# Squares of x in PSUM, the next layer's first slab on a buffer of its own, and a DRAM copy cut into eight, in a two-layer decoder kernel

## The reference

```python
def rms_norm(x, g):
    return x * rsqrt(mean(x * x, axis=-1) + EPS) * g

for layer in range(2):
    h = rms_norm(x, attn_norm[layer])
    x = x + (dsa_mixer(h, ...) if layer == 0 else swa_mixer(h, ..., sinks, ..., rel_bias))
    h = rms_norm(x, ffn_norm[layer])
    g, u = split(h @ w_gate_up[layer], 2)
    x = x + (silu(g) * u) @ w_down[layer]
out = rms_norm(x, final_norm)
```

## Time and profile before

| | us |
|---|---|
| median of 3 runs | 1193.57 (1193.28 to 1193.68) |
| profiled execution | 1198.54 |
| its span | 1196.7 |
| TensorE busy | 1166.6 (97%) |
| GpSimd busy | 613.7 (51%) |
| VectorE busy | 564.2 (47%) |
| ScalarE busy | 458.7 (38%) |

### The profile page before, as it was taken

How to read it: one execution, slowest core, us unless ns; L and a number is a source line. 1 busy time by engine, 2 the same in 40 slices (tenths; PEclk the granted TensorE clock), 3 DMA queues, 4 the chain that set the end, 5 groups by cost and what they waited for, 6 DMA issues and landing times.

```text
span 1196.7 us, 16183 instructions
## 1 busy us (share of the span) xinstructions
PE 1166.6 (97%) x5666; PEld 968.0 (81%) x5666; DVE 564.2 (47%) x931; ACT 458.7 (38%) x854; POOL 613.7 (51%) x359
## 2 busy tenths in 40 slices
PE   7999999999999999999999999999999999999997
PEld 5767889988788888888888778887888888888887
DVE  5389867644644344432222376737543444331111
ACT  5343257763423322323222376734333223322332
POOL 4435747864445444543444578824554445444441
PEclk9999999999999999999999999999999999999999
DMA  7531401118332333223332442313323332323331
GB/s 211 172 134 57 137 27 45 53 40 173 105 95 80 105 105 95 80 83 97 95 94 87 106 114 56 80 35 107 98 79 105 105 96 79 94 72 97 96 96 71
DMA packets 181571, 112.46 MB, mean 94 GB/s; under 512 B 7340, under 2 KB 175591, under 8 KB 181528
## 3 DMA queue, kind: packets, MB, share of 16 engines
q1 hardware_dynamic: 180800, 110.68, 33.2%
q10 hardware_dynamic: 728, 1.22, 0.3%
HBM read 109.72 MB, written 8.45 MB: 99 GB/s over the span
## 4 chain that ended last, share of the span: by engine, by line
PE 84%; DVE 5%; issue 2%; DMA 2%; ACT 2%; POOL 1%; ACTq 0%; SPq 0%; DVEq 0%
PE ps L576 26%; PE ps L578 26%; PE ps L577 26%; DMA raw<-in_ffn_w_gate_up 2%; PE ps L585 2%; DVE ss L1482 1%; PE ps L791 1%; DVE work L1578 1%; ACT w_hi L1090 1%; PE ps L967 1%; PE ps L770 1%; POOL w_lo L467 1%; DVE work L1562 1%; DMA raw<-in_b_w_in 1%; PE ps L970 0%
## 5 line engine op out<-in xcount | busy, mean ns | idle before, releaser
L467 POOL TENSOR_TENSOR w_lo<-raw,w_hi 128x1024 fp32r<-128x1024 f32 (+1 forms) x200 | 462.8, 2336 | 500.2 <-ACT w_hi L1090 491.7
L576 PE MATMUL ps<-xs_hi,w_hi 128*128 128x512 f32 (+3 forms) x1024 | 400.4, 391 | 8.0 <-DVE x L1678 2.9
L578 PE MATMUL ps<-xs_hi,w_lo 128*128 128x512 f32 (+3 forms) x1024 | 395.9, 387 | 0.0
L577 PE MATMUL ps<-xs_lo,w_hi 128*128 128x512 f32 (+3 forms) x1024 | 395.8, 387 | 0.0
L1090 ACT CAST w_hi<-raw 128x1024 fp32r<-128x1024 f32 (+1 forms) x196 | 178.9, 961 | 437.0 <-PE ps L578 415.6
L576 PEld LDWEIGHTS ps<-xs_hi,w_hi 128*128 128x128 f32 x1024 | 193.2, 189 | 53.6 <-issue 3.4
L577 PEld LDWEIGHTS ps<-xs_lo,w_hi 128*128 128x128 f32 x1024 | 193.3, 189 | 39.1 <-issue 1.1
L578 PEld LDWEIGHTS ps<-xs_hi,w_lo 128*128 128x128 f32 x1024 | 193.2, 189 | 39.0
L576 PE MATMUL ps<-act_hi,w_hi 128*128 128x512 f32 (+1 forms) x374 | 143.0, 382 | 0.0
L578 PE MATMUL ps<-act_hi,w_lo 128*128 128x512 f32 (+1 forms) x374 | 141.7, 379 | 0.0
L577 PE MATMUL ps<-act_lo,w_hi 128*128 128x512 f32 (+1 forms) x374 | 140.4, 375 | 0.0
(11 more groups left out here) (189 smaller groups left out, 1363.1 us busy)
## 6 DMA issues: line engine op xcount, KB each, us to landing
raw<-in_ffn_w_gate_up SPq DMA_DIRECT2D x88, 512.0 KB, 4.9
raw<-in_ffn_w_down SPq DMA_DIRECT2D x32, 384.0 KB, 3.6
raw<-in_a_w_in SPq DMA_DIRECT2D x20, 512.0 KB, 5.0
raw<-in_ffn_w_down SPq DMA_DIRECT2D x32, 320.0 KB, 4.0
raw<-in_b_w_in SPq DMA_DIRECT2D x10, 512.0 KB, 5.2
bias_toep<-bias_row SPq DMA_DIRECT2D x4, 1024.0 KB
toep<-bias_toep SPq DMA_DIRECT2D x16, 256.0 KB, 2.7
raw<-in_a_w_out SPq DMA_DIRECT2D x8, 512.0 KB, 4.1
```

Of the source, the lines that this page charges most:

```text
L467: nc.gpsimd.tensor_tensor(pieces(w_lo, n)[half], pieces(raw, n)[half], pieces(w_hi, n)[half].bitcast(F32), ALU.subtract)\
L576: nc.tensor.matmul(dst, wh, xh, start=start, stop=False, **kw)
L577: nc.tensor.matmul(dst, wh, xl, start=False, stop=False, **kw)
L578: return nc.tensor.matmul(dst, wl, xh, start=False, stop=stop, **kw)
```

## The change

- `new_x` writes the square of a tile to a PSUM bank (`NORM_SQ`, two banks for each norm) and adds from there. The very last half tiles still use `sq_mem`.
- Slab S_BK is loaded into a buffer of its own, `raw_next`, behind the tenth down slab of layer 0, and counted on a semaphore of its own. It lies over `gate`, `up` and `glu`, so its load waits for the last `act_lo`. Slab 55 takes its former slot, and waits for the split of slab 51; waits on `raw_full` of odd slabs behind S_BK count one slab less.
- The copy of the second bias table is cut into eight DMAs of two heads each (256 rows of 1 KB), one behind each of the down slabs 3 to 10 of layer 0. To that end the loop over the first five of eight output tiles (`AHEAD`) is written out on SyncE, in both layers.
- The sinks are loaded behind the first two slabs of queries.

```diff
+AHEAD = 5
+NORM_SQ = {1: (4, 5), 2: (2, 3), 3: (5, 7), 4: (2, 3)}
...
+        raw_next = sb("raw_next", [P, SLOT], F32, next_m)
...
+            if buf is raw and n == S_BK:
+                return [raw_next[:, 0:CUT_WIDE[0]], raw_next[:, CUT_WIDE[0]:CUT_WIDE[1]]]
...
             def slab(n, it, src):
                 for dst, s in src(n % 2):
-                    if n >= 2:
+                    if n == S_BK + 2:
+                        sp.wait_ge(lo_done, 2 * (S_BK - 1))
+                    elif n >= 2:
                         sp.wait_ge(lo_done, 2 * (n - 1) + 4 * it)
...
+            def row_copy(h):
+                sp.wait_ge(neg_done, 4 * H)
+                skew_b = bass.AP(tensor=bias_row.tensor, offset=h * GLEN + ROW_A + P - 1,
+                                 ap=[[GLEN, 2], [-1, P], [1, 2 * P]])
+                sp.dma_start(bias_toep[h:h + 2, :, 0:2 * P], skew_b).then_inc(toep_out, 16)
...
-                with sp.Fori(0, DM) as m:
+                for m in range(AHEAD):
+                    for c in range(2):
+                        slab(s_d + c, m, down(w_down[layer], c, m))
+                        if layer == 0 and m >= 1:
+                            row_copy(2 * (2 * (m - 1) + c))
+                if layer == 0:
+                    v = raw_next[:, :].rearrange("p (k n) -> p k n", k=DM)
+                    g = b_w_in[0].rearrange("(k p) n -> p k n", p=P)
+                    sp.wait_ge(al_done, FT)
+                    for i in range(2):
+                        sp.dma_start(v[:, 4 * i:4 * i + 4, :], g[:, 4 * i:4 * i + 4, H * DH:H * DH + 256])\
+                            .then_inc(raw_ahead, 16)
+                with sp.Fori(AHEAD, DM) as m:
                     for c in range(2):
                         slab(s_d + c, m, down(w_down[layer], c, m))
...
-            sp.wait_ge(neg_done, 4 * H)
-            skew_b = bass.AP(tensor=bias_row.tensor, offset=ROW_A + P - 1, ap=[[GLEN, H], [-1, P], [1, 2 * P]])
-            sp.dma_start(bias_toep[:, :, 0:2 * P], skew_b).then_inc(toep_out, 16)
             feed_forward(0, S_F0, S_D0)
-            slab(S_BK, 0, wide(b_w_in[0], H * DH))
-            sp.wait_ge(unit_done, U_BK)
-            sp.dma_start(sink[:, :], b_sinks[0:1, :].broadcast_to([P, H])).then_inc(sink_in, 16)
             for n in range(S_BQ, S_BO):
                 c0 = (n - S_BQ) * 2 * DH
                 slab(n, 0, two_halves(b_w_in[0], c0, c0 + H // 2 * DH))
+                if n == S_BQ + 1:
+                    sp.wait_ge(unit_done, U_BK)
+                    sp.dma_start(sink[:, :], b_sinks[0:1, :].broadcast_to([P, H])).then_inc(sink_in, 16)
...
-            sp.wait_ge(toep_out, 80)
+            sp.wait_ge(toep_out, 64 + 8 * 16)
...
-                    act.wait_ge(raw_full[n % 2], 32 * (n // 2 + 1) + 32 * it)
+                    if n == S_BK:
+                        act.wait_ge(raw_ahead, 32)
+                    else:
+                        act.wait_ge(raw_full[n % 2], 32 * (n // 2 + 1 - (n > S_BK and n % 2)) + 32 * it)
...
-                nc.scalar.activation(sq[:, par, :], x[:, m, :], ACT.Square).then_inc(sq_done, 1)
+                nc.scalar.activation(ps[:, NORM_SQ[e][par], :], x[:, m, :], ACT.Square).then_inc(sq_done, 1)
...
-                nc.vector.tensor_tensor(ss[:, :], ss[:, :], sq[:, par, :], ALU.add).then_inc(ss_done, 1)
+                nc.vector.tensor_tensor(ss[:, :], ss[:, :], ps[:, NORM_SQ[e][par], :], ALU.add).then_inc(ss_done, 1)
```

More of the change, by code:

```diff
@@ L213, in trunk @@
         act_lo = sb("act_lo", [P, FT, T], F32R, fm)
+        next_m = ExitStack()
+        raw_next = sb("raw_next", [P, SLOT], F32, next_m)
+        next_m.close()
         gate = sb("gate", [P, T], F32, fm)
@@ L230, in trunk @@
         raw_full = [sem("raw_full0"), sem("raw_full1")]
+        raw_ahead = sem("raw_ahead")
         hi_done, lo_done = sem("hi_done"), sem("lo_done")
```

## The result

The changed kernel takes 1185.41 us (median of 5, 1184.47 to 1187.31) against 1193.56 before on the same chip: a ratio of 0.9937, with a 95% interval from 0.9915 to 0.9959. That is 8.15 us less; forecast were 8.2 and 1185.3. The profiled executions lie 11.5 us apart (spans 1196.7 and 1185.2).

A forecast was written before the change was run, and what follows sets the result against it. TensorE, busy for 97% of the span, bounds the kernel, with losses at the seams between stages. Gains of 4.76 + 3.08 + 0.4 = 8.2 us off the median 1193.57 gave 1185.3 us, range 1183.6 to 1189.5.

The forecast's parts named there:

- Seam 1: Attention A to feed-forward 0: TensorE waits for x of tile 5 behind the bias copy; moving the copy gains 4.76 us.
- seam 2: Feed-forward 0 to attention B: the sinks hold up slab 54; loading them behind slabs 54 and 55 gains 3.08 us.
- seam 3: Attention B to feed-forward 1: wait of 0.5 us on the last x's low part; adding squares from PSUM gains 0.4 us.
- slow add: VectorE's add of squares beside a GpSimd split, 2.88 us; Seam 1 and seam 2 were to close even with it.
- quick add: VectorE's same add of squares, taken from PSUM: 0.69 us.
- sits there long before: Before attention B: slab 53 is in raw_next long before slab 54 lands at 661.4; no gain of its own was given.
- (c): Rival: squares gain nothing in PSUM, the add stays at 2.88 us; only 0.4 us lost, 1185.7 us; no chance given.
- The cover in the down part: Feed-forward 0's down slabs can come 10.3 us late without stalling TensorE; the copy pieces' cost taken as nothing, barely.
- backlog: Two DMA engines: piece plus down slab 7.9 to 8.4 us against 7.55; 3 to 7 us behind after eight.
- rival (f): More gain: in the stage behind seam 2 one return from the lower clock falls away, 1.7 us; 1183.6 us; 4%.

## Why the prediction was right, point by point

**The sum.** Seam 1 4.76, seam 2 3.08, seam 3 0.4: measured 4.77, 3.08 and 0.42 in the profiled executions. The total time came out 0.1 us from the forecast, which is luck: the runs scatter by more, and the kernel before had medians of 1193.79 to 1195.25 in the later comparisons.

**Where seam 1's credit belongs.** The chain that I read (copy, slab 15, cast, slow add, x of tile 5) was right link by link, and so was the claim that moving the copy closes it. The step that failed was to see only one cure: I had put the add's 2.2 us beside it ("even with the slow add"), but not asked what the quick add does while the slab stays late. The runs show that moving the copy removes the pause but for 0.26 us, and that the quick add does so too or leaves up to 0.6 us, which is all that the copy's place is then worth.

**Seam 2.** Right: the sinks alone. What I wrote of raw_next ("sits there long before") is true and worth nothing.

**The squares.** As (c) said, they matter little once the DMAs are moved: 0.26 + 0.4 us. I had seam 1's part at nothing, because I asked only whether the last add ends before the sum and left out the last low part, which is due 6 steps earlier. VectorE's timeline of before had it:

```profile
312.33 0.75 DVE L1473 SCALAR_TENSOR_TENSOR xs_lo<-x,params,xs_hi  x1 [1.18 <-ACT xs_hi L1105]
```

It ends 9.4 us after the cast at 303.71, so at 308.7 by the prediction's times, and TensorE needs it at 299.28 + 42 x 0.2275 = 308.8. That is no margin to speak of, and it came 0.26 us late.

**The cover in the down part.** The mechanism and the number of engines were right; the term for the backlog was mis-sized. During a piece the queue shows (571 to 573.5: packets, MB, share of 16 engines):

```profile
q1 hardware_dynamic: 118, 0.12, 13.6%
```

118 packets in 2.5 us on two engines: one each 42.4 ns per engine, while their busy time is 46 ns. Packets overlap by 4 ns, and I had added up busy times: 5.9 and 2.5 us instead of 5.4 and 2.1. So a cycle is 7.5 us against a period of 7.55, and no backlog grows. The tightest slab, the one behind raw_next, was asked for at 595.6 and 596.2; landings of its halves and its cast:

```profile
DMA to landing us min/median/max: 4.5/5.8/7.1
```
```profile
606.23 1.46 ACT L1119 CAST w_hi<-raw 128x768 fp32r<-128x768 f32 x2 [4.98 <-PE ps L604]
```

It was in place at 603.3, 3.1 us later than usual instead of 6 to 10, and 2.9 before its cast. With 42.5 ns in place of 46, the doubled pieces came out right too. The cut itself was not needed, as the copy left whole showed.

**Two engines, always the same.** Two heads move 48 GB/s on 2.2 engines' busy time, and the doubled pieces show that it is the same pair each time, which no row before could. The Trainium skill (DMA: Bandwidth & Descriptors, "Why a DMA increments its semaphore by 16 and not by 1") gives such a copy the lowest-numbered engines, as many up to 16 as divide the slowest dimension of both sides. The number and the sameness agree with that; that they are the lowest-numbered, no run here shows.

**The 3.3 us beyond the change** in the profiled execution. Two returns of the clock are missing in it that the trace before has: behind a wait for GpSimd at 114 us, in code that the change doesn't touch (1.6 us), and behind the pause at 767 us (1.65). The second is what rival (f) looked for in the stage behind seam 2, at the 1.7 us it named; but it isn't owed to the closed seams. Of the other ten profiled executions four show it (the kernel with only the sinks moved, and the changed one without `raw_next`, with the copy back in front and with every piece twice), three of them with seams 2 and 3 as in the changed kernel. The remainder lies within 0.1 us.

## What to carry to other kernels

When two edits shorten the same chain, price each with the other undone as well: a seam that either closes is worth its loss once, and the simpler edit may be all that is needed. Ask of each transfer in an ordered queue what it waits for, and put one that waits for a stage's end behind the loads that the next stage starts with. A copy that fits on few DMA engines leaves the others free, but everything behind it has a share on these few; count packets per engine per period, by distance of packets and not by their busy time, and compare with the cover.

## What I had not expected of the hardware

Executions of the same code fall into groups. In some, a pair of TensorE's float32 matmuls at 11 us takes 1.03 us, in others 1.89 with the same granted clock on record (1.00), and in the two shown here the program with the quick pair is 3.8 us ahead by 20 us. Timelines of the kernel with the whole copy in the down part and of the changed one:

```profile
11.24 1.03 PE L673 MATMUL ps<-hot,rel_sb 33*16 33x512 f32 x2
```
```profile
11.47 1.89 PE L673 MATMUL ps<-hot,rel_sb 33*16 33x512 f32 x2
```

The second difference is in the pause between 107 and 114 us, 2.2 us of waiting for GpSimd. In the profiled executions of three kernels (the changed one, the one with only the squares, the one with only the copy) the clock stayed up behind it; in the other nine it fell. The busy table of the kernel with the whole copy in the down part, granted clock third from the end:

```profile
111.00:114.00 3.00, 3.00 (x10) 2.32 (x9) 3.00 (x9) 1.00 (x2) 3.00 (x3) 0.58 0.13 9
```

Six steps of 0.43 us follow a first one of 0.60, 1.6 us lost in all. The Trainium skill (TensorE: Matmul & The Clock Gate, "Part 1: The HAM clock gate") says of a kernel's start that the number of matmuls before the clock rises differs from run to run of one kernel. Here, behind a pause in the same code, it differs whether the clock falls at all, and at seam 1 how long it takes to return (7 or 12 steps). Why the first matmuls differ at the same recorded clock stays open. In the changed kernel's trace the steps at 18.89 to 19.74 are also 0.43 us, as long as at the lower clock elsewhere, so the record may miss a lower clock there; no run shows it. Together with the return at 767 us the two make some 7 us, and runs of one kernel differ by up to 7.5 here. With the copy back in front they took 1184.45 to 1191.12, and the profiled one, which has all three losses, is the one of 1191.12. They are why the seams are compared by their own lengths.
